# Seven-product matrix blocks for the gates and the branch projections of two hybrid layers, with half a depthwise convolution summed in PSUM

## The reference, cut to what matters

```python
def hybrid_layer(x, ...):
    h = rms_norm(x, norm1_g)
    q, k, v, iq, ik, iw, a_in, c_in, g_in = jnp.split(h @ w_in, IN_SPLITS, axis=-1)
    ...
    y_attn = dsa_attention(q, k, v, iq, ik, iw) @ w_attn_out
    a_val, a_gate = jnp.split(a_in, 2, axis=-1)
    a = causal_dwconv(a_val * jax.nn.sigmoid(a_gate), conf_conv_w) + conf_conv_b   # 31 taps
    y_conf = jax.nn.silu(layer_norm(a, conf_ln_g, conf_ln_b)) @ w_conf_out
    c_b, c_c, c_x = jnp.split(c_in, 3, axis=-1)
    y_sc = (c_b * causal_dwconv(c_c * c_x, sc_conv_w)) @ w_sc_out                  # 3 taps
    gates = jax.nn.sigmoid(g_in.reshape(B, S, 3, D_MODEL))
    merged = gates[:, :, 0] * y_conf + gates[:, :, 1] * y_attn + gates[:, :, 2] * y_sc
    x = x + merged @ w_o
    ...                                                                            # FFN
```

## Time and profile before

| | |
|---|---|
| time, median of 3 runs | 2019.89 us (2019.89 to 2020.93) |
| the profiled execution | 2019.41 us, its span 2017.6 us |
| PE busy | 2003.7 us, 99% of the span |
| PE weight loads (overlap PE) | 1836.6 us, 91% |
| DVE / ACT / POOL busy | 1055.7 (52%) / 403.7 (20%) / 782.2 us (39%) |
| a 1 MB block of weights, issue to landing | 4.8 us |
| granted TensorE clock | nine tenths or more in all 40 slices |

### The profile page before, as it was taken

How to read it: one execution, slowest core, us unless ns; L and a number is a source line. 1 busy time by engine, 2 the same in 40 slices (tenths; PEclk the granted TensorE clock), 3 DMA queues, 4 the chain that set the end, 5 groups by cost and what they waited for, 6 DMA issues and landing times. The chain is left out here.

```text
span 2017.6 us, 34732 instructions
## 1 busy us (share of the span) xinstructions
PE 2003.7 (99%) x13230; PEld 1836.6 (91%) x13230; DVE 1055.7 (52%) x2702; ACT 403.7 (20%) x986; POOL 782.2 (39%) x537
## 2 busy tenths in 40 slices
PE   9999999999999999999999999999999999999999
PEld 7788889888889999999888888999999999899998
DVE  4244446974343567514992454557823366555541
ACT  2231521112111222111122122032202014220000
POOL 1000042000002487765000000668875774248873
PEclk9999999999999999999999999999999999999999
DMA  5314444344334455444444433444454443345444
GB/s 209 128 45 144 146 149 148 132 152 146 132 140 142 151 170 169 172 146 161 134 147 150 146 128 123 170 165 168 162 173 148 145 147 105 126 146 183 171 159 136
DMA packets 42960, 298.32 MB, mean 148 GB/s; under 512 B 4928, under 2 KB 6080, under 8 KB 8832
## 3 DMA queue, kind: packets, MB, share of 16 engines
q1 hardware_dynamic: 42560, 295.42, 42.7%
q10 hardware_dynamic: 256, 0.92, 0.3%
HBM read 294.35 MB, written 1.05 MB: 146 GB/s over the span
## 5 line engine op out<-in xcount | busy, mean ns | idle before, releaser
L708 PE MATMUL bank<-xn,ring 128*128 128x256 f32 (+2 forms) x3776 | 686.4, 340 | 0.5 <-DMA ring<-wstream 0.5
L708 PEld LDWEIGHTS bank<-xn,ring 128*128 128x128 f32 x3776 | 610.2, 190 | 69.0 <-issue 4.6
L708 PE MATMUL bank<-arena,ring 128*128 128x128 f32 (+2 forms) x3702 | 641.4, 328 | 4.3 <-DVE arena L1711 2.4
L708 PEld LDWEIGHTS bank<-arena,ring 128*128 128x128 f32 x3702 | 564.2, 191 | 62.3 <-issue 3.5
L708 PE MATMUL bank<-arena 128*128 128x128 f32 (+3 forms) x2264 | 298.1, 287 | 0.0
L708 PEld LDWEIGHTS bank<-arena 128*128 128x128 f32 (+1 forms) x2264 | 274.9, 192 | 9.3 <-issue 1.5
L708 PE MATMUL bank<-arena,h_res 128*128 128x128 f32 x1960 | 234.5, 276 | 1.9 <-POOL h_res L1676 1.2
L708 PEld LDWEIGHTS bank<-arena,h_res 128*128 128x128 f32 x1960 | 225.7, 192 | 4.5 <-POOL h_res L1676 2.4
L1711 DVE SCALAR_TENSOR_TENSOR arena<-arena,par (+2 forms) x536 | 214.6, 475 | 0.3
L1667 POOL TENSOR_TENSOR h_res<-ring 128x512 f32<-128x512 f32 x12 | 15.5, 1294 | 495.2 <-issue 363.0
L1672 POOL TENSOR_TENSOR arena<-ring 128x1024 f32<-128x1024 f32 (+1 forms) x70 | 167.0, 2385 | 89.7 <-DMA ring<-wstream 89.7
(11 more groups left out here) (224 smaller groups left out, 1624.6 us busy)
## 6 DMA issues: line engine op xcount, KB each, us to landing
ring<-wstream SPq DMA_DIRECT2D x264, 1024.0 KB, 4.8
ring<-wstream SPq DMA_DIRECT2D x16, 768.0 KB, 4.2
cst<-consts SPq DMA_DIRECT2D x1, 2488.0 KB, 14.7
h_res<-tokens SPq DMA_DIRECT2D x2, 544.0 KB, 5.3
out<-arena SPq DMA_DIRECT2D x4, 256.0 KB, 5.4
arena<-arena ACTq DMA_DIRECT2D x4, 160.0 KB, 3.8
ring<-wstream SPq DMA_DIRECT2D x2, 288.0 KB, 2.8
par<-params SPq DMA_DIRECT2D x1, 541.5 KB, 9.2
```

The lines of the kernel that those rows point to most:

```text
L708: return pe.matmul(o, lhs, rhs, start=start, stop=stop, skip_group_check=True)
```

## The change

In both middle layers:

- The 12 gate blocks become one seven-product stage `g`. The four `conf` and four `sc` blocks in the attention loop take the seven-product form too. POOL mixes their weights; DVE makes the token sums of `yc` (behind `branch_b(1)`) and of `ys` (in head 1, into `xn`).
- Tiles 0 to 3 of the 31-tap convolution stay a loop in SBUF. Tiles 4 to 7 are summed in `both_p`, in PSUM bank 4, two tiles in turn: 28 taps ahead of the gates, then eight behind each `unite` of `g` (`convolved`). While bank 4 is taken, a new kind `beside` of `take` skips it.
- ACT turns a pair of gate tiles to tanh in one operation. POOL sums the convolution's tiles beside the mixing for `g`.
- PE's order is `g`, spreads, `cx0`, mean, index products, `cx1`, variance, `cb`. DVE's order follows it: `spread_norm`, rotation of the index queries, N3 (L0), `centred`, scores, rotation of q and k, top-k, selection, the whole short convolution, the layer norm's inverse and gains, and `branch_b`, which multiplies the `cb` results straight from PSUM instead of from a copy by ACT.
- In the heads, `unite` and one gated product replace the short convolution and two gated additions.
- At the start PE runs 8 instead of 6 warm-up matmul calls.

```diff
-        pl(n + "g0", "w_in_2", l, 3, 2, 8, seq(go))
-        pl(n + "g1a", "w_in_2", l, 1, 2, 8, seq(go + 1536))
-        pl(n + "g1b", "w_in_2", l, 2, 2, 8, seq(go + 2048))
+        fast(n + "g", "w_in_2", l, 12, 1, lambda it, q: go + 256 * it)
         pl(n + "cx0", "w_in_2", l, 2, 2, 8, two(co + 1024, co + 2048))
         pl(n + "cx1", "w_in_2", l, 2, 2, 8, two(co + 1536, co + 2560))
         pl(n + "cb", "w_in_2", l, 2, 2, 8, seq(co))
-        pl(n + "conf", "w_conf_out_2", l, 2, 2, 8, seq(0))
-        pl(n + "sc", "w_sc_out_2", l, 2, 2, 8, seq(0))
+        fast(n + "conf", "w_conf_out_2", l, 4, 1, lambda it, q: 256 * it)
+        fast(n + "sc", "w_sc_out_2", l, 4, 1, lambda it, q: 256 * it)
         pl(n + "attn0", "w_attn_out_2", l, 1, 1, 8, seq(0))
         fast(n + "attn", "w_attn_out_2", l, 3, 1, lambda it, q: 256 * it + 256)
...
+        if kind == "beside":
+            self.turn["side"] += self.turn["side"] % 4 == 0
+            kind = "side"
...
+            sums_at.update({(L, "yc"): sums_of(flat(ac)), (L, "ys"): sums_of(flat(xn[:, :, :])[:, 0:16 * P])})
...
+            side = "side" if pair else "beside"
...
-            for n in range(6):
+            for n in range(8):
...
-                blocks(L + "g0", 8, x256, S)
-                blocks(L + "g1a", 8, x256, S)
-                row_spread(L + "qk", 5, 1)
+                fast_stage(F, "g", 12, 1, of_tokens(xn), (F, "x"), None)
+                row_spread(L + "qk", 5, 1, "beside")
+                blocks(L + "cx0", 8, x256, S)
                 centre_sums(L + "ln", 1, lambda j: sel[:, 0, :], [(L + "ln", "total")])
...
-                blocks(L + "cb", 8, x256, S)
+                blocks(L + "cx1", 8, x256, S)
+                b = e.take("beside", (L + "ln", "var"))
+                pe.wait_ge(*e.emptied((L + "ln", "var")))
+                for n, (event, j) in enumerate((((L + "ln", "acc"), 0), ((L + "ln", "sq", 6), 6), ((L + "ln", "sq", 7), 7))):
+                    pe.wait_ge(*e.at(event))
+                    ins = mm(b, slice(0, P), slice(0, S), C("ones"), sq[:, j, 0:S], n == 0, n == 2)
+                ins.then_inc(*e.side_done((L + "ln", "var")))
+                for q in range(4):
+                    halves(L + "cb", q, 8, [P, P], x256, S)
...
-                    if h < 4:
-                        halves(L + "conf", h, 8, [P, P], lambda k: yc[:, k, :], S)
-                        return
-                    if h == 4:
-                        for j in range(ND):
-                            pe.wait_ge(*e.at((L + "ys", j)))
-                    halves(L + "sc", h - 4, 8, [P, P], lambda k: ys[:, k, :], S)
+                    part, buf, sums = ("conf", yc, "yc") if h < 4 else ("sc", ys, "ys")
+                    fast_block((F, part, h % 4, 0), (F, part, h % 4, 0), of_tokens(buf), (F, sums),
+                               ready=[(L + "ys", j) for j in range(ND)] if h == 4 else None)
 
...
+                def gate_tanh_l(it):
+
+                    for part in ("c11", "c12", "c22"):
+                        act.wait_ge(*e.at(((F, "g", it, 0), part)))
+                    act.activation(flat(sg[:, 2 * it:2 * it + 2, :]), flat(sg[:, 2 * it:2 * it + 2, :]), ACT.Tanh,
+                                   scale=0.5).then_inc(*e.step((F, "sg", it)))
+
+                for it in range(12):
+                    first_product((F, "g", it, 0))
+                    if it >= 1:
+                        gate_tanh_l(it - 1)
+                gate_tanh_l(11)
                 for p in range(5):
...
-                act.wait_ge(*e.at((L + "yc", ND - 1)))
-                with e.turns(L + "cb", 2) as i:
-                    for q in range(2):
-                        for t in range(2):
-                            out_of((L + "cb", q, t), tile(ac, 4 * i + 2 * q + t), event=(L + "cbs", q, t))
-
...
+                      lambda h: first_product((F, "conf" if h < 4 else "sc", h % 4, 0)))
...
+                    if b[0] == L and b[1] == "g":
+                        for j in {3: (1,), 6: (2, 3), 11: (4, 5, 6, 7)}.get(b[2], ()):
+                            one = ac[:, 0, :] if j == 1 else sel[:, 0, :]
+                            event = (L + ".ln", "total") if j == 7 else (L + ".ln", "part", j)
+                            pool.wait_ge(*(e.at_turn((L + ".ac",), j // 2) if j < 4 else e.at((L + ".ac", j))))
+                            pool.tensor_tensor(out=sel[:, 0, :], in0=one, in1=ac[:, j, :], op=ALU.add).then_inc(*e.step(event))
+                            pool.wait_ge(*e.at(event))
+                    if b == (L, "g", 11, 0):
+                        gather(L + ".ln", S, sq)
...
-                with e.turns(L + "conv", 4) as i:
+                with e.turns(L + "conv", 2) as i:
...
+                def convolved(lo, hi):
+
+                    for n in range(lo, hi):
+                        j, k = 4 + 2 * (n // (2 * CK)) + n % 2, n % (2 * CK) // 2
+                        acc, weight = both_p[:, n % 2, :], G(g("conf_conv_w_2"), CK * j + k)
+                        if k == 0:
+                            if n >= 2 * CK:
+                                dve.wait_ge(*e.at((L + "ac", j - 2)))
+                            dve.tensor_scalar(acc, cp[:, j, 0:S], weight, G(g("conf_conv_b_2"), j), ALU.mult,
+                                              ALU.add).then_inc(*e.step((L + "tap", j, k)))
+                        else:
+                            dve.wait_ge(*e.at((L + "tap", j, k - 1)))
+                            stt(ac[:, j, :] if k == CK - 1 else acc, cp[:, j, k:k + S], weight, acc, ALU.mult,
+                                ALU.add).then_inc(*e.step((L + "ac", j) if k == CK - 1 else (L + "tap", j, k)))
+
+                convolved(0, 28)
                 rows_inverse(L + "qk")
...
+                for it in range(12):
+                    unite((F, "g", it, 0), sg[:, 2 * it:2 * it + 2, :], 0)
+                    convolved(28 + 8 * it, 36 + 8 * it)
...
                 spread_norm(L + "qk", 5, lambda p: g("q_norm_g_2" if p < 4 else "k_norm_g_2"), qk0, qk0, L + "qkn")
-                centred(L + "ln", 8, lambda j: ac[:, j, :])
...
+                centred(L + "ln", 8, lambda j: ac[:, j, :])
...
+                def branch_b(q):
+
+                    for t in range(2):
+                        j, key = 2 * q + t, (L + "cb", q, t)
+                        dve.wait_ge(*e.at(("pe", key)))
+                        dve.wait_ge(*e.at((L + "sct", j, 2)))
+                        dve.tensor_tensor(ys[:, j, :], psum[e.bank_of(key)][:, 0:S], ys[:, j, :],
+                                          ALU.mult).then_inc(*e.frees(key, (L + "ys", j)))
+
...
+                short_conv(0)
+                short_conv(1)
+                dve.wait_ge(*e.at((L + "ln", "rms")))
...
+                branch_b(0)
+                for j in range(ND):
+                    dve.wait_ge(*e.at((L + "zt", j)))
+                    stt(yc[:, j, :], ac[:, j, :], 1.0, yc[:, j, :], ALU.add, ALU.mult).then_inc(*e.step((L + "yc", j)))
+                branch_b(1)
+                for j in range(ND):
+                    dve.wait_ge(*e.at((L + "yc", j)))
+                token_sums((F, "yc"), yc)
+                branch_b(2)
+                branch_b(3)
+
                 def branches_part(h):
 
+                    if h == 1:
+                        for j in range(ND):
+                            dve.wait_ge(*e.at((L + "ys", j)))
+                        token_sums((F, "ys"), ys)
                     if h == 0:
-                        for q in range(2):
-                            for t in range(2):
-                                dve.wait_ge(*e.at((L + "cbs", q, t)))
-                    if h < 4:
-                        for t in range(2):
-                            j = 2 * h + t
-                            dve.wait_ge(*e.at((L + "scp", j)))
-                            dve.tensor_scalar(ys[:, j, :], scp[:, j, 0:S], G(g("sc_conv_w_2"), 3 * j), None,
-                                                 ALU.mult).then_inc(*e.step((L + "tap", j, 0)))
...
+                    n, part = (h - 1) % 4, "conf" if h <= 4 else "sc"
+                    tiles = slice(2 * n, 2 * n + 2)
+                    gate = sg[:, 2 * n + (0 if h <= 4 else 16):2 * n + (2 if h <= 4 else 18), :]
+                    unite((F, part, n, 0), both_p, 0, *([(F, "branch", h - 1)] if h > 1 else []))
+                    dst = mg[:, tiles, :] if h <= 4 else tmp[:, 0:2, 0:S]
+                    dve.wait_ge(*e.at((F, "sg", n + (0 if h <= 4 else 8))))
+                    stt(dst, gate, 1.0, both_p, ALU.add, ALU.mult).then_inc(*e.step((F, "branch", h)))
+                    dve.wait_ge(*e.at((F, "branch", h)))
+                    if h > 4:
+                        dve.tensor_tensor(mg[:, tiles, :], mg[:, tiles, :], dst, ALU.add).then_inc(*e.step((F, "merged", n)))
+                        dve.wait_ge(*e.at((F, "merged", n)))
```

(24 more changed lines are left out.)

126 lines of the change are left out of this document (41 added, 85 removed).

## The result

The changed kernel takes 2036.35 us (median of 4 runs, 2033.97 to 2039.48) against 2020.24 us before. The ratio is 1.0082, with a 95% interval of 1.0067 to 1.0097: slower by 0.8%, where I had forecast 2017.6, and outside my range (2009 to 2026).

What follows compares the result with a forecast made beforehand. TensorE, busy for nearly the whole span, was taken to bound the kernel. Profiled 2019.41 - 25.0 gain + 22.2 waits + 0.5 start = 2017.1, with the median 0.5 higher 2017.6 us; range 2009 to 2026.

Steps and rivals of the forecast that it cites:

- The gain: Seven-product gates, conf and sc blocks shorten PE's own work by 12.5 us per middle layer, 25.0 for both.
- The pace of `g`: Gate stage: 6.25 us per block, with POOL and DVE (unite plus eight taps, 5.2) keeping up.
- Wait a: Spreads behind g: the fourth waits for spread_norm, behind unite and eight taps on DVE; 3.3 us per layer.
- Wait b: At cb 2: PE waits for DVE's 51.0 us chain from the mean; 3.3 us per layer, bounds 1 to 6.
- Wait c: Head 1's transposes wait for the sums of ys, slowed by POOL's mixing; 4.2 us, bounds 0.9 and 6.3.
- Heads 5 to 7: Attention heads with one more two-SBUF operation on DVE: 0.1 us of wait each, 0.3 per layer.
- Start: Start of the kernel: two more start-up matmuls, partly inside the wait for the first weights, cost 0.5 us.
- the sum: Both middle layers: the waits and heads 5 to 7 add up to 22.2 us, giving back nearly all the gain.
- Rival 4: Whole kernel: the whole gain comes through, all three waits hidden, 1995.4 us; chance 0.06.

Runs made afterwards that it cites:

- e5: The changed kernel with the edits of e2, e3 and e4 together: 1994.20 us, ratio 0.9874.
- e2: The changed kernel with the five spread_norm operations ahead of the last eight convolution taps instead of behind them: 2028.04 us, ratio 1.0033.
- e1: The changed kernel with matmuls that compute nothing needed put into its three waits per middle layer (6, 8 and 12 calls): 2021.95 us, ratio 1.0005.
- e3: The changed kernel with the mean taken in the middle of cx0 and ScalarE's eight squares put behind the relu operations: 2019.52 us, ratio 0.9998.
- e7: The changed kernel with GpSimd starting its mixing for conf 2 only when the four sums of ys are done: 2028.25 us, ratio 1.0042.
- e4: The changed kernel with the four token sums of ys put one by one behind the normalisations of heads 0 to 3: 2019.99 us, ratio 0.9997.
- e8: The changed kernel with filling matmuls only before the transposes of head 1 (12 calls): 2033.05 us, ratio 1.0068.
- e9: The changed kernel with filling matmuls only at the fourth index product (8 calls): 2027.61 us, ratio 1.0037.

## Why the prediction was wrong, point by point

- **The gain** was right: 12.5 per layer forecast, 13.3 by the trace, and e5 delivers it whole.
- **The pace of `g`** was right: 6.26 per block, eight taps in PSUM at 3.23 (forecast 3.4), no wait.
- **Wait a**: 3.3 forecast, 2.99 measured, cause and place as said; e2 shows the cause.
- **Wait b**: 3.3 forecast, 4.18 and 4.08 measured, but the wait that showed is another one. I had put it down to the long DVE chain to `cb` 2, with the index products as a remark. What PE waited for is ScalarE's eight squares ahead of the relu operations, the last ones paced by a subtraction each. My chain was of the right length, 50.7 in e1 against 51.0, and PE only came late enough to `cb` 2 because it had already stood still at the index products. What I missed is that two waits stood one behind the other and the first hides the second; e3, with its two edits, takes away both.
- **Wait c**: 4.2 forecast, 6.37 and 6.18 measured, the cause as said. The sums took 7.6 where I took 6.1 from one group in the earlier trace rows; the other group there (8.2) was nearer. The normalisation, 1.45 with its reciprocals, was 0.4 over the 1.05 that I took. e7 sizes the contention in place at 4.2, and e4 the whole. It came out just above my upper bound of 6.3. I had also read the sum from 754.26 as outlasting the POOL operation by the length of one sum; it is 757.16 - 756.61 = 0.55, and one sum takes 0.69.
- **Heads 5 to 7**: 0.3 per layer forecast, nothing measured (7.89 per turn throughout).
- **Start**: 0.5 forecast, nothing measured in the two profiled executions: `g` of layer 0 begins at 388.28, and the first gate block before began at 388.24.
- **The step that failed is the sum**: 2 x (3.3 + 3.3 + 4.2 + 0.3) counted a wait at its idle time. The idle time alone was 26.8 against my 22.2, 4.6 off. The larger part, 15.7 by the trace and 14.4 by e1, is the half clock behind the waits, and no term, bound or rival had it. The trace of the kernel before could not show it: its longest rest of PE, 2.41 us in stage A, was followed by full clock. But six new waits of 3 to 6 us had no like in it either, and I took their price for known. The length of the stages behind them needed a term, or a rival. With my own three waits and that share, 2017.6 + 15.7 = 2033.3, which is slower by 0.7%.
- **Rival 4** (the whole gain, 1995.4) is what e5 measures, 1994.2: the arithmetic of the form was right, and the kernel had merely not been arranged for it.

What stays open: why one rest of 2 to 3 us is followed by the half clock and another, of the same length at the same place, isn't.

## What to carry to other kernels

Where TensorE is never idle, a new wait can cost more than its length: allow for a stretch at half clock behind each, here 0 to 5 us lost, and read it from the length of equal stages rather than from the list of waits. Ask too what the wait hides: with it gone, PE comes earlier to the next place and can meet the next late engine there. When an edit speeds TensorE up, look for short work on another engine that could move a few us: three small moves turned a loss of 0.8% into a gain of 1.3%. If a wait can't be removed, matmuls into a bank that will be overwritten can buy back the clock, as in e1.

## What the runs showed that I had not expected

- Useless matmuls in the waits made the program 14.4 us faster.
- The price of one wait isn't fixed. The rest of 2.98 to 2.99 at the fourth spread was followed by spreads of 1.99 or 2.00 and `cx0` of 27.79 in some places and executions, and by 2.41 and 29.10 (changed kernel, layer 0) or 2.73 and 28.78 (e8, layer 0) in others. The same wait lost nothing or 1.5 to 1.7 us, and in each of six profiled executions (changed kernel, e3, e4, e7, e8, e9) it lost that in one layer and nothing in the other. The changed kernel's runs spread over 5.5 us, e5's over 2.6; this may be a part of it.
- It isn't a matter of the change. Stage A has a rest of 2.41 to 2.43 in every kernel here, the one before included. In six of the eleven traces the stage behind it takes 33.91, in the other five (e1, e2, e3, e7, e8) 35.54 or 35.59, and where I looked, in e1, the clock falls to 0.59 just behind the rest. First before, then e1:

```profile
239.87 33.91 PE L708 MATMUL bank<-arena,ring 128*128 128x256 f32 x156 [2.41 <-DVE arena L1711]
```

```profile
240.22 35.59 PE L714 MATMUL bank<-arena,ring 128*128 128x256 f32 x156 [2.43 <-DVE arena L1721]
```

- Behind the wait for the index products the clock was at 0.50 for the whole window from 507.0 to 512.3, and `cx1` behind it lost another 1.3 to 2.6.
- Taps with their sum in PSUM kept 0.42 each while POOL mixed, and sums with both operands in SBUF went from 0.69 to as much as 2.73. Three taps on DVE and the mixing beside them on POOL in the changed kernel:

```profile
454.68 1.27 DVE L1705 SCALAR_TENSOR_TENSOR bank<-arena,par,bank 128x256 f32<-128x256 f32 x3
454.99 1.27 POOL L1670 TENSOR_TENSOR arena<-arena,ring 128x512 f32<-128x512 f32 x1
```
